# Queries and keys of both attentions token-major, normed by one number per token and head, and turned on TensorE

## What is computed

```python
h = rmsnorm(x, g_mix)
proj = h @ w_in            # fox q,k,v (8 heads x 128), forget logits, LRU x and gate, memory q, merge gates
q = rmsnorm(fq per head, g_q_fox);  k = rmsnorm(fk per head, g_k_fox)
y_fox = softmax(q k^T * 128**-0.5 + c_i - c_j, causal) @ v       # c = cumsum(log_sigmoid(forget logits))
y_lru = rg_lru(conv(lx)) * gelu(lg)
mk, mv = split(rmsnorm(mem, g_mem) @ w_mem_kv)                    # 256 memory tokens
qm = rmsnorm(mq per head, g_q_mem); km = rmsnorm(mk per head, g_k_mem)   # 4 heads x 256
y_mem = softmax(qm km^T * 256**-0.5) @ mv
x = x + (sum over the 3 branches of sigmoid(gates) * (y @ w_branch)) @ w_out
out = x + conv_geglu(rmsnorm(x, g_ffn))                           # FFN_HIDDEN 5632
```

## Time and profile before

| | us |
|---|---|
| median of 3 runs | 1657.31 (1656.4 to 1659.15) |
| the profiled execution, its own time | 1657.26 |
| its span, first to last instruction | 1655.6 |
| PE busy | 1639.1 (99%) |
| DVE busy | 1117.0 (67%) |
| ACT busy | 893.2 (54%) |
| POOL busy | 55.8 (3%) |

### The profile page before, as it was taken

The page is one execution under the profiler, slowest core; times in us unless marked ns, Lnnn a source line. Parts: engine busy times, 40 slices in busy tenths (PEclk is TensorE's granted clock), DMA queues, the critical chain, the costliest instruction groups (busy, mean ns, idle before and its releaser), DMA issues.

```text
span 1655.6 us, 27015 instructions
## 1 busy us (share of the span) xinstructions
PE 1639.1 (99%) x9226; PEld 1419.2 (86%) x9226; DVE 1117.0 (67%) x1323; ACT 893.2 (54%) x1138; POOL 55.8 (3%) x57
## 2 busy tenths in 40 slices
PE   9999999999999999999999999999999999999998
PEld 7788888888888888888888888888888888888887
DVE  6976678778757466565666777777777777545443
ACT  6766667466645455445455555555555555433332
POOL 0010121000000000000001000000000000000000
PEclk9999999999999999999999999999999999999999
DMA  8545455644455555555555555555555555655553
GB/s 319 191 140 168 156 173 189 209 161 139 166 190 189 191 181 190 190 188 189 183 192 184 181 181 196 192 188 181 199 181 179 198 193 188 198 196 196 203 197 101
DMA packets 85256, 307.35 MB, mean 186 GB/s; under 512 B 9880, under 2 KB 10656, under 8 KB 85088
## 3 DMA queue, kind: packets, MB, share of 16 engines
q1 hardware_dynamic: 83952, 302.88, 55.0%
q0 software_dynamic: 1120, 3.94, 0.7%
q10 hardware_dynamic: 144, 0.01, 0.0%
HBM read 304.69 MB, written 2.11 MB: 185 GB/s over the span
## 4 chain that ended last, share of the span: by engine, by line
PE 90%; DVE 5%; DMA 2%; issue 2%; ACT 1%; SPq 0%; POOL 0%; ACTq 0%; DVEq 0%; POOLq 0%
PE psG L335 87%; PE psM L335 2%; DVE W L937 2%; DMA raw<-w_units 1%; DVE fox_rstd L967 1%; DMA xs<-xT 1%; ACT W L599 1%; DVE X L1124 0%; DMA lru_rg<-w_rg 0%; DVE x_n L1220 0%; PE psM L444 0%; ACT fox_rstd L638 0%; DVE fox_S L995 0%; DVE stat L998 0%; DVE sq L1167 0%
## 5 line engine op out<-in xcount | busy, mean ns | idle before, releaser
L335 PE MATMUL psG<-X,W 128*128 128x512 f32 (+1 forms) x5632 | 993.7, 338 | 2.9 <-DVE X L1124 2.9
L335 PEld LDWEIGHTS psG<-X,W 128*128 128x128 f32 x5632 | 860.6, 188 | 131.4 <-issue 5.7
L937 DVE TENSOR_TENSOR W<-raw,W 128x1024 fp32r<-128x1024 f32 x566 | 686.4, 1227 | 318.2 <-ACT W L599 315.5
L599 ACT ACTIVATE W<-raw 128x1024 fp32r<-128x1024 f32 x566 | 590.0, 1054 | 317.3 <-PE psG L335 309.1
L335 PE MATMUL psG<-hidden,W 128*128 128x512 f32 (+1 forms) x1408 | 245.4, 337 | 0.0
L335 PEld LDWEIGHTS psG<-hidden,W 128*128 128x128 f32 x1408 | 214.0, 188 | 31.3
L607 ACT ACTIVATE low<-psG 128x512 f32<-128x512 f32 x132 | 79.0, 598 | 216.4 <-PE psG L335 216.4
L335 PE MATMUL psG<-Y,W 128*128 x768 | 134.4, 337 | 0.0
L335 PEld LDWEIGHTS psG<-Y,W 128*128 128x128 f32 x768 | 117.0, 188 | 17.1
L1367 DVE SCALAR_TENSOR_TENSOR up_c<-up_pad,par_sb,up_c 128x256 f32<-128x256 f32 x176 | 77.5, 482 | 42.3 <-ACT up_c L881 36.3
L335 PE MATMUL psG<-merged,W 128*128 128x512 f32 (+1 forms) x512 | 89.3, 337 | 0.0
(11 more groups left out here) (190 smaller groups left out, 681.1 us busy)
## 6 DMA issues: line engine op xcount, KB each, us to landing
raw<-w_units SPq DMA_DIRECT2D x566, 512.0 KB, 3.4
xs<-xT SPq DMA_DIRECT2D x4, 512.0 KB, 8.9
outT<-xs POOLq DMA_DIRECT2D x7, 256.0 KB, 3.4
mem_raw<-first_data SPq DMA_DIRECT2D x3, 512.0 KB, 5.3
mem_raw<-memT SPq DMA_DIRECT2D x3, 512.0 KB, 8.3
lru_rg<-w_rg POOLq DMA_DIRECT2D x8, 128.0 KB, 4.2
c_all<-c_rows POOLq DMA_DIRECT2D x1, 1024.0 KB, 5.5
outT<-xs SPq DMA_DIRECT2D x2, 128.0 KB, 1.8
```

The lines of the kernel that those rows point to most:

```text
L335: return nc.tensor.matmul(*a, skip_group_check=True, **kw)
L599: nc.scalar.activation(W[:, s, :, 0], raw[:, s], ACT.Copy).then_inc(hi_done, 1)
L937: V.tensor_tensor(W[:, s, :, 1], raw[:, s], f32(W[:, s, :, 0]), ALU.subtract).then_inc(lo_done, 1)
```

## The change

Memory keys (`mk`, units 16 to 31), memory queries (`mq`, 32 to 47) and fox keys and queries (`kq`, 96 to 127, in turn keys and queries of four heads) become wide groups: token-major, 512 columns. 64 units change from narrow to wide. The norm of a head is then one number per token: ACT squares a head's columns straight from `psG` and sums them along the row with the same instruction (`norm_squares`: 8 instructions for a fox group, 4 for a memory group), takes one root of a few columns, DVE inverts it and multiplies the whole group out of `psG` (`norm`). TensorE turns the result into channel-major with 8 transposes a group (`turn`, hook 1 of the next group: after its second unit), and ACT copies it out with the gain (`turned_copied`). There are 8 such groups (`NORMED`). The matmuls with ones (`sums`) are gone, so are `add_squares` and `stage_values` on POOL and the wide reciprocals. The memory's 1/rms enters the key norm through its epsilon (`mem_eps`) and the values through the copied softmax weights. Memory attention now handles two heads at a time, in two rounds in place of four. `scores` moves from hook 4 to 3 and the softmax one offset earlier for memory heads on both engines, for fox on ACT. All memory products come first, so X is first needed at unit 32; x is scaled and split in the steps at units 25 to 29. The fox rounds 2 and 3 lie in `gate0`. The loops over `mkq` and `qk` are written out. The first gate DMA of the LRU (`load_gates`) may be issued when unit 31 is done, before at unit 48. Sync's queue is unchanged.

```diff
-PHASES = [("mv", 1, 2, 8, 512), ("mkq", 4, 2, 4, 256), ("lru", 4, 2, 4, 256), ("v", 1, 2, 8, 512), ("qk", 4, 2, 4, 256)]
+PHASES = [("mv", 1, 2, 8, 512), ("mk", 1, 2, 8, 512), ("mq", 1, 2, 8, 512), ("lru", 4, 2, 4, 256), ("v", 1, 2, 8, 512),
+          ("kq", 1, 4, 8, 512)]
...
+NORMED = [("mk", 0), ("mk", 1), ("mq", 0), ("mq", 1), ("kq", 0), ("kq", 1), ("kq", 2), ("kq", 3)]
+NORM_GROUP = [G0[_name] + _w for _name, _w in NORMED]
...
+            def turn(j, **banks_free):
+
+                def hook():
+                    if j == 0:
+                        pe.wait_ge(const_in, 48)
+                        pe.wait_ge(root_done, 1)
+                    else:
+                        pe.wait_ge(turned_out, j)
+                    side_waits(**banks_free)
+                    pe.wait_ge(evac_done, NORM_GROUP[j] + 1)
+                    for d in range(4):
+                        for t in range(2):
+                            o = d % 2 * T + t * P
+                            ins = nc.tensor.transpose(psM[:, d // 2, o:o + P], normed[:, t, d * P:(d + 1) * P], ident[:])
+                    ins.then_inc(turned, 1)
+                return hook
...
-                def sums():
-                    if kind == "fox":
-                        side_waits(act=side_count(kind, m, "act", "squares"))
-                        for j in range(2):
-                            ins = mm(psM[:, j, :], ones[:], A["S"][:, j].rearrange("p a t -> p (a t)"), start=True, stop=True)
-                    else:
-                        side_waits(pool=side_count(kind, m, "pool", "squares_added"))
-                        ins = mm(psM[:, 0, :].rearrange("p (j t) -> p j t", j=2), ones[:], A["S"][:, :, 0], start=True, stop=True)
-                    done(ins)
+                last_turn = {"mem": [2, 3], "fox": [5, 6, 7, 7]}[kind][m]
+                own_turn = {"mem": [2, 3], "fox": [5, 5, 7, 7]}[kind][m]
 
                 def scores():
-                    side_waits(dve=side_count(kind, m, "dve", "normed"))
+                    pe.wait_ge(turned_out, own_turn + 1)
+                    side_waits(dve=side_count(kind, m, "dve", None), act=side_count(kind, m, "act", None))
...
-                return {0 if kind == "fox" else 1: sums, 4: scores, 6: transposes, 7: values}
+                return {3: scores, 6: transposes, 7: values}
...
-            mkq(None, {7: mem_sums})
-            with pe.Fori(1, 4) as i:
-                mkq(i, attention_hooks("mem", i - 1))
-            plain("lru", None, attention_hooks("mem", 3))
+            wide_group("mk", 0, m_op, {0: mem_sums, 4: x_sums})
+            wide_group("mk", 1, m_op, {1: turn(0)})
+            x_ready = lambda n: pe.wait_ge(xX_lo, n // 2 + 1)
+            wide_group("mq", 0, x_op, {1: turn(1)}, ready=x_ready)
+            wide_group("mq", 1, x_op, {1: turn(2), **attention_hooks("mem", 0)})
+            plain("lru", None, {1: turn(3, act=side_count("mem", 0, "act", "weights_copied")), **attention_hooks("mem", 1)})
             with pe.Fori(1, 4) as i:
                 plain("lru", i, lru_hooks(i - 1))
             wide_group("v", 0, x_op, lru_hooks(3))
             wide_group("v", 1, x_op, decay_hooks())
-            plain("qk", None, {})
-            with pe.Fori(1, 4) as i:
-                plain("qk", i, attention_hooks("fox", i - 1))
-            plain("gate0", None, attention_hooks("fox", 3))
+            wide_group("kq", 0, x_op, {})
+            wide_group("kq", 1, x_op, {1: turn(4, dve=side_count("decay", 0, "dve", "z"))})
+            wide_group("kq", 2, x_op, {1: turn(5), **attention_hooks("fox", 0)})
+            wide_group("kq", 3, x_op, {1: turn(6, act=side_count("fox", 0, "act", "weights_copied")), **attention_hooks("fox", 1)})
+            plain("gate0", None, {1: turn(7, act=side_count("fox", 1, "act", "weights_copied")), **attention_hooks("fox", 2)})
+            plain("gate0", 1, attention_hooks("fox", 3))
...
+            def norm_squares(kind, j):
+
+                g = NORM_GROUP[j]
+                phase, w = NORMED[j]
+                heads = 4 if phase == "kq" else 2
+                d = 2 * UC // heads
+                squared = square["fox" if phase == "kq" else "mem"]
+                act.wait_ge(pe_units, GROUPS[g][3] + 1)
+                for t in range(2):
+                    for h in range(heads):
+                        ins = nc.scalar.activation(squared[:, t, h * d:(h + 1) * d], psG[:, 2 * (w % 2) + t, h * d:(h + 1) * d], ACT.Square,
+                                                   accum_out=head_ss[:, t, h:h + 1])
+                ins.then_inc(head_squares, 1)
+                act.wait_ge(head_squares, j + 1)
+                if j > 0:
+                    act.wait_ge(evac_done, NORM_GROUP[j - 1] + 1)
+                if phase == "mk":
+                    act.wait_ge(mem_eps_set, 1)
+                    for t in range(2):
+                        ins = nc.scalar.activation(head_rms[:, t, 0:2], head_ss[:, t, 0:2], ACT.Sqrt, bias=mem_eps[:, t:t + 1])
                 else:
-                    src, dst, bias = psM[:, 0:2, :], A["rstd"].rearrange("p j a t -> p j (a t)"), eps[:, 2:3]
-                done(nc.scalar.activation(dst, src, ACT.Sqrt, bias=bias))
+                    bias = eps[:, 1:2] if phase == "mq" else eps[:, 2:3]
+                    ins = nc.scalar.activation(head_rms[:, :, 0:heads], head_ss[:, :, 0:heads], ACT.Sqrt, bias=bias)
+                ins.then_inc(head_root, 1)
+
+            def turned_copied(kind, j):
+                phase, w = NORMED[j]
+                act.wait_ge(turned, j + 1)
+                src = psM[:, 0:2, :].rearrange("p h (d t) -> p h d t", d=2)
+                if phase == "kq":
+                    dst = att["fox"]["qT" if w % 2 else "kT"][:, 4 * (w // 2):4 * (w // 2) + 4].rearrange("p (h d) t -> p h d t", d=2)
+                    ins = nc.scalar.activation(dst, src, ACT.Copy, scale=p1("g_q", 0) if w % 2 else gk_s[:, 0:1])
+                else:
+                    dst = att["mem"]["qT" if phase == "mq" else "kT"][:, 4 * w:4 * w + 4].rearrange("p (h d) t -> p h d t", d=2)
+                    for d in range(2):
+                        ins = nc.scalar.activation(dst[:, :, d], src[:, :, d], ACT.Copy,
+                                                   scale=p1("g_qm", d) if phase == "mq" else gkm_s[:, d:d + 1])
+                ins.then_inc(turned_out, 1)
...
+                    act.wait_ge(mem_rstd, 1)
+                    for kt in range(2):
+                        ins = nc.scalar.activation(A["PT"][:, :, kt], psM[:, 0:2, kt * T:(kt + 1) * T], ACT.Copy,
+                                                   scale=rstd_tok[:, kt:kt + 1])
+                done(ins)
...
-            softmax = {8: [exp], 10: [weights_copied], 11: [attention_hi]}
-            steps_at = {"mem": {3: [squares], 5: [root], **softmax}, "fox": {3: [squares], 4: [root], **softmax},
+            softmax = {7: [exp], 10: [weights_copied], 11: [attention_hi]}
+            steps_at = {"normed": {3: [norm_squares], 5: [turned_copied]}, "mem": softmax, "fox": softmax,
...
+                if 9 <= u < 13:
+                    c = u - 9
+                    if c == 0:
+                        act.wait_ge(first_in[2], 16)
+                    nc.scalar.activation(sq0["mem"][:, c], mem_raw[:, 4 * c:4 * c + 4], ACT.Square).then_inc(sq_done["mem"], 1)
+                if 13 <= u < 17:
+                    c = u - 13
+                    act.wait_ge(x_in[c], 16)
+                    nc.scalar.activation(sq0["x"][:, c], xs[:, 4 * c:4 * c + 4], ACT.Square).then_inc(sq_done["x"], 1)
...
+                if u == 34:
                     act.wait_ge(lam_dve, 1)
                     nc.scalar.activation(lam_t["e"][:], lam_t["t"][:], ACT.Exp, scale=-1.0).then_inc(lam_act, 1)
-                if u == 25:
+                if u == 35:
                     act.wait_ge(lam_dve, 2)
                     nc.scalar.activation(lam_t["l"][:], lam_t["u"][:], ACT.Ln).then_inc(lam_act, 1)
-                if u == 16:
+                if u == 20:
+                    act.wait_ge(mem_ss, 1)
+                    root_mean_square(rstd_tok[:], psM[:, 2, 0:2]).then_inc(mem_root, 1)
+                if u == 24:
                     act.wait_ge(ss_done, 1)
-                    root_mean_square(rstd0[:, 1], psM[:, 0, 0:T]).then_inc(root_done, 1)
-                if u == 27:
-                    act.wait_ge(ss_done, 2)
-                    root_mean_square(rstd0[:, 0], psM[:, 1, 0:T])
-                    root_mean_square(rstd_tok[:], psM[:, 2, 0:2]).then_inc(root_done, 1)
-                if 20 <= u < 24:
-                    c = u - 20
+                    root_mean_square(rstd_x[:, 0], psM[:, 0, 0:T]).then_inc(root_done, 1)
+                if 26 <= u < 30:
+                    c = u - 26
                     act.wait_ge(x_scaled, c + 1)
                     gained_hi(X, x_n, "g_mix", range(4 * c, 4 * c + 4)).then_inc(xX_hi, 1)
 
...
-            def norm_k(kind, m):
```

(79 more changed lines are left out.)

271 lines of the change are left out of this document (106 added, 165 removed).

## The result

The changed kernel takes 1647.88 us (median of 5 runs, 1647.22 to 1650.49) against 1657.53 for the kernel before (5 runs on the same chip): 9.65 us less. The ratio of their runs is 0.9944, 95% interval 0.9931 to 0.9956. The forecast was 1649.8, 7.5 less. The mechanism was the one forecast; the waits at the turns were put some 3 us too high, a fall of the granted clock that cost 1.6 us was not in the sum, and smaller terms were off too, so that the forecast came within some 2 us partly by luck.

What follows compares the result with a forecast made beforehand. PE, busy 99% of the span, was taken as the bound. From 1657.3 us: -4.2 (wide) -10.7 (sums) +7.6 (turns) -8.7 (waits gone) +8.5 (turns late) = -7.5, so 1649.8; range 1642 to 1659.

Steps and rivals of the forecast that it cites:

- PE is the bound, all else only through its waits: Whole kernel: PE busy in 99% of the span, so time comes off only by taking work or waits from PE.
- Wide units: 64 units going from narrow to wide save 0.065 us each on PE through 4 fewer instructions: 4.2 us less.
- Sums: Matmuls with ones removed from four fox rounds, four memory rounds and partly at the start: 10.7 us less on PE.
- Turns: 64 added 128x128 transposes on PE, eight in each of eight turns: 7.6 us more, bounds 7.0 to 9.0.
- Waits that go: PE's waits for X, POOL, softmax weights, LRU weights and a low half at the start vanish: 8.7 us less.
- The 0.7 at the start: PE's wait for a unit's low half goes, as ACT squares memory at units 7 to 10: 0.7 us less.
- Turns late: PE waits at six turns for the norm chain over ACT and DVE: 8.5 us more, bounds 3 to 12.
- that turns aren't late: Rival: cheaper squares or a PE trailing its records leave 2 us of the turn waits, 1643.3; chance 0.15.
- a unit behind: Rival: ACT not caught up at group ends, chain 2.72 us later, 18.5 us of turn waits, 1668.3; chance 0.12.
- The loads aren't dearer: Rival denied here: each table switch holds ACT another 1.28 us, adding 6.5 at turns 1, 4, 6, 7, 1656.3; chance 0.06.

Runs made afterwards that it cites:

- e4: Changed kernel with the low-half product of the 64 widened units issued as two matmuls of 256 columns, 16 matmuls a unit: 1652.38 us.
- e7: Kernel before the change with each matmul of ones that sums squares over partitions issued twice: 1665.38 us.
- e2: Changed kernel with the eight roots of the head norms replaced by an Identity, which needs no table load: 1644.04 us.
- e3: Changed kernel with every turn's eight transposes issued twice into the same place: 1655.49 us.
- e9: Changed kernel with only turn 0 one unit later: 1645.97 us.
- e5: Changed kernel with all eight turns one unit earlier, behind the first unit of the next group: 1674.92 us.
- e1: Changed kernel with turns 0, 1 and 4 one unit later, behind the third unit of the next group: 1640.56 us.

## Why the prediction was right, and where it was off

- **PE is the bound, all else only through its waits**: right. DVE lost 52 us of work and POOL 17, which by themselves bring nothing; what counted is 9.75 us on PE.
- **Wide units**, 4.2: measured 64 x 0.062 = 4.0; the cause, fewer instructions, is shown by e4.
- **Sums**, 10.7: 0.86 to 1.72 a round, 10.3 together, doubled one for one in e7; the 0.4 of the sum at the start is part of what changes before unit 16. Right as PE time.
- **Turns**, 7.6: five at 0.87 and three, behind a wait, at 1.06 (turn 1 by e2, where the clock stays up): 7.5; e3. The dearer row, 0.14 for a transpose, held a hidden wait: the same six take 0.66 once nothing is late.
- **Waits that go**, 8.7: the waits for X (2.9), POOL (2.4), the softmax weights (1.7) and the LRU (1.0) went. The 0.7 at the start did not: PE now waits 0.6 for the copy of `mem_v` there. On the other side, waits cost more than their rows show. The softmax wait had 0.8 more in the transposes' pieces. The piece behind each of the others was longer than without a wait: 3.03 for 2.79 at both waits for X, 1.13 for 0.86 behind POOL, 1.99 for 1.73 behind the LRU's weights, 1.0 together. So 9.8 went.
- **Turns late**, 8.5: this is the term that was mis-sized, and the step in it is the price of the squares. Measured, in turns 0 to 7: 2.3, 2.1, 0, 0, 1.0, 0, 0, 0; forecast 2.4, 2.3, 0, 0, 2.0, 0.7, 0.6, 0.5. Turns 0 to 3, which hang on no fox squares, were right to 0.2, turn 1 with some luck: its memory squares took 1.6 where 2.0 was worked out, and its roots and the step from DVE to PE (0.14) were priced too low. The fox group's eight squares were priced by exponentials, 0.40 each, and follow after 0.25: at turn 4 they took 2.2 us (331.68 to the load at 333.86) and not 3.2, which is all of the error there and more than the waits forecast for turns 5 to 7.
- **Not in the sum**: the fall of the clock after turn 1, 1.6 us (e2, e9). The prediction doesn't mention PE's clock.
- **The rivals**: that turns aren't late, for squares cheaper than exponentials, was true in part: it took 3.0 of the 8.5. ACT was not a unit behind (it waited 1.66 for the group's end), and e5, which makes the chain a unit late for PE, shows what that rival would have cost: 17.2 in waits, where 18.5 was worked out, and 26.6 with the clock. The loads aren't dearer: e2 gives 1.28 back for one. The drain of about 1.38 us on top of each, which the Trainium skill counts (ScalarE: Activation LUTs, What ACT_TABLE_LOAD costs), isn't seen in this kernel: at turn 4 the load ends at 335.14 and the root starts at 335.15.

Why a square is cheaper than the exponential that stood for it is read from rows of the changed kernel, and no run tests it. Both rows below read 256 columns out of PSUM and sum them:

```profile
102.32 0.37 ACT L650 ACTIVATE mem_square<-psG 128x256 f32<-128x256 f32 x1
102.68 0.37 ACT L650 ACTIVATE mem_square<-psG 128x256 f32<-128x256 f32 x1
...
142.76 0.46 ACT L689 ACTIVATE mem_S<-psM,stat 128x256 f32<-128x256 f32 x1
143.21 0.47 ACT L689 ACTIVATE mem_S<-psM,stat 128x256 f32<-128x256 f32 x1
```

From one start to the next it is 0.36 us for the square and 0.45 for the exponential. The exponential has a bias per partition (`stat`), the square none. The Trainium skill (ScalarE: Activation LUTs, What ACT_TABLE_LOAD costs) says that each such operand adds about 93 ns; the traces agree, with 0.09. Of the 0.15 between a fox square and its exponential that leaves 0.06. The fox exponentials read SBUF and the squares PSUM, which fits some 0.04 of it: for 256 columns the exponential out of SBUF took 0.49, out of PSUM 0.45.

The account up to unit 143, less time first: -4.0 (wide), -10.3 (sums), +7.5 (turns), -8.0, -0.8 and -1.0 (waits gone, with what was hidden behind them), +5.5 (turns late), +1.6 (clock), -0.4 (the start, unit 16 begins at 51.53 and before at 51.89) = -9.9, against 9.75 measured.

## What to carry to other kernels

Where one engine is busy all the time, a hook on it should stand not where its data may be ready but where it surely is: one unit later cost nothing here, and standing early cost 7.6 us of a possible 17.3 (e1). Before placing it, add up the chain in the queues of the other engines, with what they do for others in the same step (x and lambda in turns 0 and 1). Price an instruction by a row of the same operands, not only of the same shape; and a wait can hide in the piece behind it, so doubling a suspected cost measures the cost less the wait that takes it up.

## What was unexpected in the hardware

The granted clock falls to 1.2 GHz after some idle stretches of PE of about 2 us. Over the profiled executions of the changed kernel and the experiments on it, once the clock had risen at the start: stretches up to 1.04 us were never followed by a fall, those of 3.8, 4.8 and 5.0 us (e5) always; between 1.8 and 2.5 both occur. At turn 0, 2.1 and 2.3 us were not followed by one (the changed kernel, e2, e3, e4); at turn 1, 1.9 and 2.1 us were (the changed kernel, e3, e4, e9); in e5, 1.84 at turn 2 and 2.48 at turn 5 were not, 2.39 and 2.38 at turns 6 and 7 were. In the kernel before, 2.4 us were not.

The same kernel doesn't have the same falls in every execution. Two of the ten runs of e3 have a mean granted clock of 1.0, the others 0.997 to 0.999, and these two are the fastest, 1653.45 and 1653.82 against 1655.18 to 1656.85. That is about the 1.6 us of one fall. The changed kernel has 0.998 in the three runs of 1647.22 to 1647.88 and 0.997 in those of 1649.5 and 1650.49. So the medians carry part of a fall more or less, and a difference of 1 or 2 us between two of them can be that alone. What decides whether a fall comes these runs don't show. A fall lasted 3.4 or 6.8 us in these traces, and one of 3.4 cost 1.6 us, nearly as much as the wait before it.
